# Mixture-of-experts weight streaming: one 2 MB gate-up transfer per expert in place of two 1 MB halves

## The reference, cut to what matters

```python
def moe(h, lp):
    B, T, D = h.shape
    t = h.reshape(B * T, D)
    ...
    gu = jnp.einsum('nd,edf->nef', t, lp['w_exp_gu'])
    a = jax.nn.silu(gu[..., :EXPERT_FF]) * gu[..., EXPERT_FF:]
    a = (a * combine[..., None].astype(a.dtype)).reshape(-1, N_EXPERTS * EXPERT_FF)
    routed = a @ lp['w_exp_down'].reshape(N_EXPERTS * EXPERT_FF, D_MODEL)
    sgu = t @ lp['w_sh_gu']
    shared = (jax.nn.silu(sgu[:, :SHARED_FF]) * sgu[:, SHARED_FF:]) @ lp['w_sh_down']
    return (routed + shared).reshape(B, T, D)
```

## Time and profile before

| | |
|---|---|
| median of 3 runs | 2201.86 us |
| lowest and highest of them | 2197.17 and 3838.0 us |
| time of the profiled execution | 2202.68 us |
| its span, from the first to the last instruction | 2200.9 us |
| busy: PE, PEld, DVE, ACT, POOL | 86%, 64%, 59%, 47%, 22% of the span |
| granted TensorE clock, mean of the span | 0.933 of full speed |
| bytes moved by DMA | 417.82 MB, 190 GB/s over the span |

### The profile page before, as it was taken

How to read it: one execution, slowest core, us unless ns; L and a number is a source line. 1 busy time by engine, 2 the same in 40 slices (tenths; PEclk the granted TensorE clock), 3 DMA queues, 4 the chain that set the end, 5 groups by cost and what they waited for, 6 DMA issues and landing times. The chain is left out here.

```text
span 2200.9 us, 27147 instructions
## 1 busy us (share of the span) xinstructions
PE 1899.9 (86%) x9234; PEld 1403.2 (64%) x9234; DVE 1303.8 (59%) x1857; ACT 1039.3 (47%) x1709; POOL 491.5 (22%) x430
## 2 busy tenths in 40 slices
PE   4999999899987599998639989979999777998992
PEld 2887556788875266666438865668887635666661
DVE  2255556544445588888753455575444365888885
ACT  2332235523333277777533422464323524877772
POOL 0003310400000434534200042114000023454540
PEclk7999999999997699999959999989999887999996
DMA  7544463233325299999834435403334235999994
GB/s 249 169 131 129 136 231 116 64 123 117 133 71 195 82 324 347 340 345 343 295 112 149 131 110 175 153 6 105 128 121 143 115 114 200 350 354 343 341 329 172
DMA packets 145062, 417.82 MB, mean 190 GB/s; under 512 B 26160, under 2 KB 36688, under 8 KB 118864
## 3 DMA queue, kind: packets, MB, share of 16 engines
q1 hardware_dynamic: 124208, 376.54, 49.3%
q0 software_dynamic: 17952, 33.74, 4.8%
q10 hardware_dynamic: 2816, 6.39, 0.8%
HBM read 409.70 MB, written 32.15 MB: 201 GB/s over the span
## 5 line engine op out<-in xcount | busy, mean ns | idle before, releaser
L1587 DVE TENSOR_TENSOR W_split<-W,W_split 128x2048 fp32r<-128x2048 f32 (+2 forms) x92 | 216.0, 2350 | 420.9 <-ACT W_split L1215 420.9
L2097 PE MATMUL psum<-W_split,qT_split 128*128 128x512 f32 (+3 forms) x1536 | 411.2, 380 | 16.2 <-PEq L2393 8.0
L1215 ACT ACTIVATE W_split<-W 128x2048 fp32r<-128x2048 f32 (+2 forms) x92 | 170.0, 1854 | 382.1 <-PE psum L2097 382.1
L2097 PEld LDWEIGHTS psum<-W_split,qT_split 128*128 128x128 f32 x1536 | 284.5, 190 | 71.8 <-issue 16.5
L2097 PE MATMUL psum<-W_split,scratch_split 128*128 128x512 f32 x864 | 279.7, 395 | 0.0
L2097 PE MATMUL psum<-W_split,hT_split 128*128 128x512 f32 x576 | 212.5, 396 | 5.8 <-DVE scratch_split L1782 5.8
L2340 PE MATMUL psum<-W_split,zf_split 128*96 128x512 f32 x512 | 204.2, 399 | 0.0
L2097 PEld LDWEIGHTS psum<-W_split,scratch_split 128*128 128x128 f32 x864 | 161.7, 188 | 38.4
L2097 PE MATMUL psum<-W_split,kT_split 128*128 128x512 f32 (+3 forms) x480 | 177.5, 370 | 0.0
L2097 PEld LDWEIGHTS psum<-W_split,hT_split 128*128 128x128 f32 x576 | 108.3, 188 | 31.5 <-DVE scratch_split L1782 6.3
L1137 POOL COPY vm<-vm 96x1 uint32 x64 | 64.2, 1003 | 252.3 <-ACT zf L1488 252.3
(11 more groups left out here) (341 smaller groups left out, 3982.3 us busy)
## 6 DMA issues: line engine op xcount, KB each, us to landing
W<-in_w_exp_gu SPq DMA_DIRECT2D x128, 1024.0 KB
W<-in_w_exp_down SPq DMA_DIRECT2D x64, 1024.0 KB
W<-in_w_in SPq DMA_DIRECT2D x60, 1024.0 KB, 5.1
W<-in_w_mod SPq DMA_DIRECT2D x40, 1024.0 KB, 5.2
W<-in_w_br SPq DMA_DIRECT2D x16, 1024.0 KB, 5.1
zf<-y_rows SPq DMA_DIRECT2D x12, 1024.0 KB, 7.0
W<-in_w_out SPq DMA_DIRECT2D x8, 1024.0 KB, 5.0
W<-in_w_mod SPq DMA_DIRECT2D x3, 2048.0 KB, 18.7
```

The source lines that it names most:

```text
L1215: nc.scalar.activation(high(j), piece(SPLITS[j]), ACT.Copy).then_inc(S["high_ready"], 1)
L1587: V.tensor_tensor(piece(SPLITS[j], Wr), piece(SPLITS[j]), high(j).bitcast(F32), ALU.subtract).then_inc(S["low_ready"], 1)
L2097: ins = nc.tensor.matmul(bank(job, piece_size(key)[1]), act_part[:, k0 + k, t * P:(t + 1) * P], w_part[:, k, :], start=first and (k, i) == ...
```

## The change

The gate-up weights of an expert come in one transfer of 128 partitions x 16 KB. The load waits until the whole gate-up of the previous tile in that slot has been multiplied, so the semaphore `gu_half` goes, and the four landing semaphores of the halves become two. The shared expert's gate-up weights are loaded in one transfer as well. ACT still rounds, DVE still subtracts and TensorE still multiplies half by half; both roundings now wait for the same landing. The number of the expert is read after the wait for the whole gate-up.

```diff
                     def load_gate_up(s, src):
-                        for h in range(2):
-                            load_half(s, h, src)
-
-                    def load_half(s, h, src):
-                        sp.dma_start(gu_half(s, h), src.rearrange("(p k) n -> p k n", p=P)[:, 4 * h:4 * h + 4, :]).then_inc(S[f"gu_landed{s}{h}"], 16)
+                        sp.dma_start(expert_gu(s), src.rearrange("(p k) n -> p k n", p=P)).then_inc(S[f"gu_landed{s}"], 16)
...
-                    for h in range(2):
-                        sp.dma_start(gu_half(1, h), rows(a["w_sh_gu"], l)[h * D // 2:(h + 1) * D // 2].rearrange("(k p) n -> p k n", p=P)
-                                     ).then_inc(S[f"gu_landed1{h}"], 16)
+                    sp.dma_start(expert_gu(1), rows(a["w_sh_gu"], l).rearrange("(k p) n -> p k n", p=P)).then_inc(S["gu_landed1"], 16)
...
-                    sp.sem_inc(S["gu_half"], 2)
-                    sp.wait_ge(S["gu_half"], 3)
-                    load_half(0, 0, expert("w_exp_gu", 2))
                     sp.wait_ge(*filled(("gu", 0)))
-                    load_half(0, 1, expert("w_exp_gu", 2))
+                    load_gate_up(0, expert("w_exp_gu", 2))
...
                             if not (last and e == 1):
-                                sp.wait_ge(S["gu_half"], tile + 4)
-                                src = expert("w_exp_gu", expert_of(tile + 3))
-                                load_half(1 - e, 0, src)
                                 sp.wait_ge(*job_filled(turn, e, "gu"))
-                                load_half(1 - e, 1, src)
+                                load_gate_up(1 - e, expert("w_exp_gu", expert_of(tile + 3)))
...
                     def gu_high(e, h, landed_at):
 
-                        act.wait_ge(S[f"gu_landed{e}{h}"], landed_at)
+                        act.wait_ge(S[f"gu_landed{e}"], landed_at)
                         nc.scalar.activation(gu_wide(e, h), gu_half(e, h), ACT.Copy).then_inc(S["gu_high"], 1)
...
-                    pe.wait_ge(S["gu_landed10"], 16)
-                    pe.wait_ge(S["gu_landed11"], 16)
+                    pe.wait_ge(S["gu_landed1"], 16)
...
-                            ins.then_inc(S[("gu_half", "psum_filled")[h]], 1)
+                        ins.then_inc(S["psum_filled"], 1)
```

More of the change, by code:

```diff
@@ L393, in trunk @@
         names += [f"y_landed{i}" for i in range(3)]
-        names += ["dec_scaled", "mixture_rows", "post_root", "pre_root", "x_cleared", "halves_used", "high_ready", "low_ready", "h_split", "oT_high", "mgT_high", "x_high", "gu_high", "gu_low", "gu_half", "a_high", "dn_high", "dn_low"]
-        landed_names = [f"piece_landed{i}" for i in range(RAW)] + ["gu_landed00", "gu_landed01", "gu_landed10", "gu_landed11", "dn_landed0", "dn_landed1"]
+        names += ["dec_scaled", "mixture_rows", "post_root", "pre_root", "x_cleared", "halves_used", "high_ready", "low_ready", "h_split", "oT_high", "mgT_high", "x_high", "gu_high", "gu_low", "a_high", "dn_high", "dn_low"]
+        landed_names = [f"piece_landed{i}" for i in range(RAW)] + ["gu_landed0", "gu_landed1", "dn_landed0", "dn_landed1"]
         sems = [nc.alloc_semaphore(n) for n in names + landed_names]
```

## The result

The changed kernel takes 2317.45 us (median of 4 runs, 2299.88 to 2320.1), against 2203.9 us for the kernel before beside it: a ratio of 1.0513, 95% interval 1.0473 to 1.0553. It is slower, as forecast, but by 114 us where 81 were forecast; 2317 lies 5 us above the range. The ratio leaves out one execution of the kernel before, which took 3838 us. Three later measurements of the changed kernel, on other chips, gave 1.0487 [1.0443, 1.0531], 1.0501 [1.0462, 1.0540] and 1.0523 [1.0497, 1.0550]. The profiled execution took 2319.47 us, its span is 2317.7 us.

The account below looks back on a forecast made before the run. The prediction took a serial chain of transfer and engines in the expert loops as the bound. Engines 10.95 + 1.00 + 2.26 = 14.2 plus transfer 9.0 gave 23.2 us a round, +81 us, 2284 us; range 2240 to 2312.

Parts of the forecast that it names:

- What bounds: Expert loops of both layers: a round of two experts is 9.35 us of transfer and 10.95 of engines in series.
- the signs named: Changed kernel's profile: gate-ups 11.6 us apart, ACT waiting before first halves, DMA share near 0.85 at some 305 GB/s.
- Term 1, later issue: SP in the expert loops: wait, number read and issue follow the whole gate-up, adding 1.00 us to a round's engine part.
- Term 2, first half no longer ahead: ACT and DVE in the expert loops: half 0 starts only when all has landed, adding 2.26 us to a round.
- Term 3, the transfer: Gate-up load in the expert loops: the 2 MB transfer takes 9.0 us, with the queue in front of it empty.
- my bounds of 7.6 and 9.35: 2 MB gate-up transfer: 7.6 us at the full rate, 9.35 us at the loop's rate beside gathers and scatters.
- The doubling that I had named: PE in the loops: added pauses of 1.5 us an expert could lower the clock and double the gate-up; given little chance.
- The single transfer: Gate-up weights in one 2 MB transfer: the prediction gave its form no cost of its own.
- Faster: Rival: long runs and one transfer fewer an expert raise the streams' rate, 47 us less, 2155 us; chance 0.04.
- Hidden: Rival: loops are bound by bytes, so a later issue only shortens the queue; within 2%, transfer 7.8 us or less; chance 0.14.
- Much slower: Rival: down load ahead in the queue or long runs delaying gathers and scatters; 1.5 us a round gives 2329; chance 0.12.

Follow-up runs that it names:

- late halves: Kernel before, with both 1 MB halves issued after the whole gate-up and the expert's number read after the wait: 2232.62 us, 1.0132.
- both landed: Kernel before, with the rounding of half 0 waiting until both halves have landed, issues unchanged: 2251.93 us, 1.0215.
- product between: Kernel before, with the older expert's silu and hidden product moved between the newer weights' two halves: 2194.41 us, 0.9972; the same in the changed kernel: 2260.4 us, 1.0273.
- clock kept up: Changed kernel, with two added fp32 matmuls into an unused bank in each TensorE step, ahead of the wait for the hidden product: 2304.5 us, 1.0467.

## Why the prediction was right, and where it fell short

**What bounds.** Right. ACT's wait moved to the first halves, the round is a transfer and a chain in series, and parting the change shows both lengthenings at work, the first of them bundled with the later read. Of the signs named, the DMA share and rate came out lower than I said (0.80 and 295 GB/s for 0.85 and 305), and the gate-ups 12.0 us apart for 11.6.

**Term 1, later issue.** Right. From the start of the product to the issue it is 2027.77 - 2019.90 = 7.87 us, before 6.79: +1.08 for a forecast of 1.00 (+0.84 in the mean over loads 3 to 29). Reading the number early gave 24 us back, 0.8 a round.

**Term 2, first half no longer ahead.** Right. From the landing to the product 2019.90 - 2013.55 = 6.35, before 4.16: +2.19 for 2.26. The whole turn is 14.22 us where I had 14.2. In the run that waits for both halves alone the way from the landing to the product is 6.37 in the mean too.

**Term 3, the transfer.** 8.8 in the mean for a forecast of 9.0, but not for the reason given. I held that the queue in front of the load would be empty, with the down load some 9 us ahead. But the gate-up loads alternate: one goes out some 9.4 us after the other slot's, 6.5 us after its down load, which takes 8.8 us to land; the next some 14 us after. The first kind took 9.1 and 9.3 us in the mean of the two loops, the second 8.5 and 8.5. So near half of the loads still meet the down load of the other slot. The experiments show this as a give-back: +1.8 of engines brought -0.7 of transfer (late halves), +2.5 brought -1.0 (both landed), and in the other direction -2.9 brought +2.5 (product between). The mean stayed within my bounds of 7.6 and 9.35; single transfers reached 11.6. That the term came out within 0.2 us is in part luck.

**The step that failed** stands in the rivals: "the clock in the loop is 0.99 and its pauses short, so I give that little". I took the added pauses as 1.5 us an expert, evenly. They come as 3 to 4.5 us ahead of every other gate-up and bring the lower level for a part of it. The doubling that I had named was too strong; the mean gate-up went from 5.84 to 6.5. The engine part is 15.1 and 15.0 us in place of 14.2, so +0.85 x 30 = 25 us, less 5 for the shorter transfer: 102 us over both loops against 81. In the means over loads 3 to 29 the longer gate-ups are 0.68 of it. The way from the hidden product to the gate-up adds 0.27 (1.17 for 0.90), since ahead of every other gate-up TensorE is still at the tile before. Both go back when the clock is kept up (5.85 and 0.96). Against this the two forecast terms came out 0.07 and 0.16 us smaller in the mean, and the engine part before was 11.08 in the mean where my one turn had 10.95. The trace before had the price in small: two gate-ups inside its loops took 7.2 and 7.3 us, after its two longest pauses, 2.15 and 2.34. What I can't claim is that the clock alone costs 25 us, since with the clock kept up the transfer took half of it back.

**Outside the rounds** I forecast nothing, and the profiled execution has 14.7 us there. The last interval of each loop, gate-up 30 to 31, is 10.7 and 12.8 us for 8.6 and 8.7, together 6; 0.9 lies ahead of the first loop. The remaining 8 are mostly in the stretch between the loops, 762.8 us for 757.7. Over all kernels run here this stretch was 754.6 to 762.8, without clear order by what was changed, so I take it for scatter and leave it open. Either alone, the 20 us in the rounds or the 15 outside them, would have left the time inside the range; it took both to pass it.

**The single transfer.** I wrote that the form costs nothing by itself. With issue and landing equal, one transfer of 2 MB is 0.7% slower than two of 1 MB: its transfers measure 0.7 to 0.8 us longer from the last issue, 0.5 of which is that the first of two goes out 0.5 us before the last. The rule of the Trainium skill, "SBUF — State Buffer", section "The DMA setup-cost knee", that a DMA-bound stream should go in the largest transfers, brought nothing here: the trend is against it, by a little (1.0501 for one transfer, 1.0427 for two).

**The rivals.** "Faster" is refuted: in no kernel did the larger transfer bring time, and what would have had to be 6.1 us or less was 8.8. "Hidden" named a real mechanism, the give-back, but it wanted a transfer of 7.8 us or less, and the mean is 8.8. "Much slower" gave 2329 for 1.5 us more a round, and the kernel came to lie between it and the forecast.

## What to carry to other kernels

Splitting a transfer in two is worth more by what it lets begin early, at both ends, than it costs: here an issue before the slot is free as a whole, the number read ahead of it, and a rounding before all has landed were together worth 4.4% of 5.1. In a loop of transfer and engines in series, write down both parts of the round: what is added to the engines is paid for by about half or more, what is taken from them is taken back by the queue as soon as the DMA engines stand at 0.97 of their time. And where two slots alternate, look at each slot's pauses by itself before calling them short, and read register values ahead of a wait, not behind it.

## What the runs showed of the hardware that I had not expected

- Two transfers of 64 partitions x 16 KB in place of two of 128 x 8 KB, with the same bytes, brought the loop to 175 GB/s at a DMA share of 0.98 and the kernel to 1.23 times its time.
- After a pause of 3.5 us on PE, 24 matmuls took 7.1 us for 5.6 (granted clock 0.76 over them); before, with all but two pauses in the loops under 2 us, the loop held 0.99. Slow gate-ups also came after pauses of 1.7 us, and fast ones after 3.4.
- With the read of a register behind the wait the issue came 1.0 us after the last matmul in the mean, 0.2 with the read ahead of it.
- Packets of 16 KB took about 0.61 us and those of 8 KB about 0.31 (medians, worked out from the traces): the longer run brought no higher rate.
